# Memory attention of a two-layer hybrid model: products of rounded operands in place of fp32 ones, values of a head for 512 queries at once

## The reference, cut to what matters

```python
MEM_HEADS = 4; MEM_HEAD_DIM = 256

def memory_attention(h, m, w_q, w_k, w_v, w_o):
    b, s, _ = h.shape
    ml = m.shape[1]
    q = (h @ w_q).reshape(b, s, MEM_HEADS, MEM_HEAD_DIM)
    k = (m @ w_k).reshape(b, ml, MEM_HEADS, MEM_HEAD_DIM)
    v = (m @ w_v).reshape(b, ml, MEM_HEADS, MEM_HEAD_DIM)
    sc = jnp.einsum('bqhd,bkhd->bhqk', q, k).astype(jnp.float32) * (MEM_HEAD_DIM ** -0.5)
    pr = jax.nn.softmax(sc, axis=-1).astype(v.dtype)
    o = jnp.einsum('bhqk,bkhd->bqhd', pr, v).reshape(b, s, D_MODEL)
    return o @ w_o

x = x + memory_attention(rmsnorm(x, norm_mem_q[i]), rmsnorm(mem, norm_mem_kv[i]), w_mq[i], w_mk[i], w_mv[i], w_mo[i])
```

## Time and profile before

| | before |
|---|---|
| median of 3 runs | 3662.88 us (3661.35 to 3664.59) |
| the profiled execution, its time | 3663.21 us |
| its span, first to last instruction | 3661.4 us |
| TensorE busy (matmul) | 3595.0 us, 98% |
| VectorE busy | 2130.7 us, 58% |
| ScalarE busy | 1832.3 us, 50% |
| GpSimd busy | 1836.9 us, 50% |
| mean granted clock of TensorE | 0.996 |

### The profile page before, as it was taken

One profiled execution on the slowest core, in us unless ns is written; L12 is line 12 of the kernel. 1 busy time (PEld: TensorE's weight loads), 2 busy tenths in 40 slices (PEclk: granted clock), 3 DMA queues, 4 the chain that ended last, 5 costly groups with the idle time before them and its releaser, 6 DMA issues.

```text
span 3661.4 us, 58169 instructions
## 1 busy us (share of the span) xinstructions
PE 3595.0 (98%) x19482; PEld 2943.8 (80%) x19482; DVE 2130.7 (58%) x3276; ACT 1832.3 (50%) x3521; POOL 1836.9 (50%) x1579
## 2 busy tenths in 40 slices
PE   9999999999999989999999999999999999999999
PEld 7877788888887767888888887788888997678887
DVE  6576642788635766427886664742236977743234
ACT  5656444444445664444434645844445753754443
POOL 3424573556544245735555763265564235245563
PEclk9999999999999999999999999999999999999999
DMA  4211241465322112414653422132223552012222
GB/s 150 91 64 41 81 144 58 161 192 188 104 91 86 65 41 82 145 62 160 191 191 113 139 92 93 59 104 95 94 97 112 176 173 81 2 58 90 95 97 87
DMA packets 106912, 388.58 MB, mean 106 GB/s; under 512 B 11856, under 2 KB 11984, under 8 KB 106320
## 3 DMA queue, kind: packets, MB, share of 16 engines
q1 hardware_dynamic: 87840, 318.81, 26.2%
q10 hardware_dynamic: 16416, 57.62, 4.7%
...
...
## 4 chain that ended last, share of the span: by engine, by line
PE 74%; issue 13%; POOL 7%; DVE 3%; ACT 1%; DMA 0%; POOLq 0%; DVEq 0%; ACTq 0%
PE ps L713 18%; PE ps L715 18%; PE ps L714 18%; POOL arena_parts L656 4%; PE ps L1215 2%; PE ps L2522 2%; PE ps L2545 2%; POOL arena_parts L666 2%; PE ps L2510 1%; PE ps L1234 1%; PE ps L1223 1%; POOL lines L440 1%; PE ps L1193 1%; PE ps L978 1%; PE ps L956 1%
## 5 line engine op out<-in xcount | busy, mean ns | idle before, releaser
L714 PE MATMUL ps<-arena_parts 128*128 128x512 f32 (+1 forms) x3148 | 1171.3, 372 | 0.0
L656 POOL TENSOR_TENSOR arena_parts<-ring,arena_parts 128x512 fp32r<-128x512 f32 x506 | 671.1, 1326 | 805.0 <-ACT arena_parts L633 798.6
L666 POOL TENSOR_TENSOR arena_parts<-ring,arena_parts 128x512 fp32r<-128x512 f32 x506 | 684.5, 1353 | 294.1 <-ACT arena_parts L642 293.3
L713 PE MATMUL ps<-h_parts,arena_parts 128*128 128x512 f32 x2080 | 814.6, 392 | 1.4 <-DVE arena_parts L563 1.2
L715 PE MATMUL ps<-h_parts,arena_parts 128*128 128x512 f32 x2080 | 809.4, 389 | 0.0
L1872 DVE SCALAR_TENSOR_TENSOR conv<-ps,cols,conv 128x511 f32<-128x511 f32 (+3 forms) x536 | 377.5, 705 | 535.2 <-ACT conv L1887 387.3
L714 PEld LDWEIGHTS ps<-arena_parts 128*128 128x128 f32 x3148 | 594.4, 189 | 104.1 <-issue 2.4
L633 ACT ACTIVATE arena_parts<-ring 128x512 fp32r<-128x512 f32 x574 | 360.2, 628 | 605.2 <-PE ps L715 572.8
L642 ACT ACTIVATE arena_parts<-ring 128x512 fp32r<-128x512 f32 x574 | 359.9, 627 | 590.2 <-PE ps L715 549.2
L713 PEld LDWEIGHTS ps<-h_parts,arena_parts 128*128 128x128 f32 x2080 | 390.5, 188 | 86.1 <-issue 3.3
L715 PEld LDWEIGHTS ps<-h_parts,arena_parts 128*128 128x128 f32 x2080 | 390.5, 188 | 81.7
...
## 6 DMA issues: line engine op xcount, KB each, us to landing
...
```

What stands on the lines that cost most here:

```text
L656: eng.tensor_tensor(side_of(lin, i, c, 0, to), side_of(lin, i, c, 0, raw), side_of(lin, i, c, 0, top), ALU.subtract)\
L666: eng.tensor_tensor(side_of(lin, i, c, 1, to), side_of(lin, i, c, 1, raw), side_of(lin, i, c, 1, top), ALU.subtract)\
L713: pe.matmul(out, w_h, x_h, start=start, stop=False)
L714: pe.matmul(out, w_h, x_r, start=False, stop=False)
```

## The change

1. Keys, values, queries and turned probabilities are held as high part (fp32r) and rest. ScalarE's copies write the high part and count `m_high`; VectorE then makes the rest from PSUM and counts `lin_free` (`memory_rest_dve`). The rests lie in space that is free at the time (`hc`, `sq`, `arena`, `conv`).
2. Scores of a unit are 2 x `three` products of 256 columns. A unit's turned probabilities are copied by ScalarE as high part, and VectorE makes the rest (`rest_of_prob`, new semaphore `pt_rest`).
3. The values of a head are made once for its 512 queries: 4 x `three` products of 512 columns, when its last block is turned and split, in TensorE's step n = 5, 9, 13 (heads 0, 1, 2). Before, they were made for each unit.
4. The scores of units 0 and 1, their softmax and the first normalisation run ahead of the last query chunk (`mem_first_*`). Unit 2's scores wait until all eight query chunks have their rest.
5. The values of head 3 stand in `mo`'s first chunk, ahead of k = 6.

```diff
-        m_q = cut(4096, KD, SEQ)
-        m_k = cut(8192, KD, MEM)
-        m_v = cut(10240, 2, DM)
+        m_q, mq_rest = cut_parts(4096, KD, SEQ), cut_parts(12288, KD, SEQ)
+        m_k, mk_rest = cut_parts(8192, KD, MEM), hc_parts
+        m_v, mv_rest = cut_parts(10240, 2, DM), sq_parts[:, :, :].rearrange("p a b -> p (a b)").rearrange("p (t n) -> p t n", t=2)
+        m_probT = [(cut_parts(16384, 2, SEQ), cut_parts(17408, 2, SEQ)), (conv_parts[:, 0:2, :], conv_parts[:, 2:4, :])]
...
+        def mem_scores(pe, l, un):
+
+            wait(pe, "p_done", un.at - 1)
+            pe.wait_ge(S["lin_free"], L["mq", l].chunk0 + 2 if un.nth % MEM_UNITS < 2 else L["mq", l].freed)
+            for c in range(2):
+                k = 2 * un.hd + c
+                mm = three(pe, un.scores, m_q[:, k, un.qs], mq_rest[:, k, un.qs], m_k[:, k, :], mk_rest[:, k, :], c == 0, c == 1)
+            mm.then_inc(S["sc_done"], 1)
+
+        def mem_values(pe, l, hd):
+
+            pe.wait_ge(S["pt_ready"], U_MEM[l] + (hd + 1) * QB)
+            pe.wait_ge(S["pt_rest"], l * MEM_UNITS + (hd + 1) * QB)
+            if hd >= 2:
+                pe.wait_ge(S["mo_evac"], l * MEM_HEADS + hd - 1)
+            p_high, p_rest = m_probT[hd % 2]
+            for c in range(2):
+                cs = slice(hd * 256 + c * P, hd * 256 + (c + 1) * P)
+                for kb in range(2):
+                    mm = three(pe, ps[:, 2 * (hd % 2) + c, :], m_v[:, kb, cs], mv_rest[:, kb, cs], p_high[:, kb, :], p_rest[:, kb, :], kb == 0, kb == 1)
+            mm.then_inc(S["pv_done"], QB)
...
+            for n, un in enumerate(units):
+                if n > QB and n % QB == 1:
+                    mem_values(pe, l, n // QB - 1)
+                if n + 2 < MEM_UNITS:
+                    mem_scores(pe, l, units[n + 2])
+                turn(un)
...
+            def rest_of_prob(un):
+                dve.wait_ge(S["pt_ready"], un.at + 1)
+                dve.tensor_tensor(un.rest, un.turned, un.high.bitcast(F32), ALU.subtract).then_inc(S["pt_rest"], 1)
...
+            for n in range(1, MEM_UNITS + 2):
+                if 2 <= n < MEM_UNITS:
+                    mem_top_dve(dve, units[n])
+                if 2 <= n <= MEM_UNITS:
+                    mem_inverse_dve(dve, units[n - 1])
+                if n >= 2:
+                    rest_of_prob(units[n - 2])
+                if n >= 2 * QB and n % QB == 0:
+                    out(n // QB - 2)
             out(MEM_HEADS - 1)
...
+            for n in range(1, MEM_UNITS + 1):
+                if 2 <= n < MEM_UNITS:
+                    mem_exps_act(act, units[n])
+                copy(units[n - 1])
+                if n >= 7 and n % QB == 3:
+                    out(n // QB - 1)
             out(MEM_HEADS - 1)
...
-                linear_pe(pe, L["mq", l], pair_of(HP, rest_of(rest_mq)), SEQ, n["mq"].split, after=banks_of(L["mv", l], MEM // P))
-                att_pe(pe, mem_pass(l), 0, 0, 0, True, True)
-                linear_pe(pe, L["mo", l], pair_of(of(o_high), HP), SEQ, lambda k: [("mo_evac", l * MEM_HEADS + max(k // 2, MEM_HEADS - 2) + 1)])
+                linear_pe(pe, L["mq", l], pair_of(HP, rest_of(rest_mq)), SEQ, n["mq"].split, after=banks_of(L["mv", l], MEM // P),
+                          hook=hooks(c5=lambda: mem_first_pe(pe, l)))
+                mem_pe(pe, l)
+                linear_pe(pe, L["mo", l], pair_of(of(o_high), HP), SEQ, lambda k: [("mo_evac", l * MEM_HEADS + max(k // 2, MEM_HEADS - 2) + 1)],
+                          midway=(KD - 2, lambda: mem_values(pe, l, MEM_HEADS - 1)))
...
-                split_dve(dve, n["mq"], X, lambda k: col(("mq_norm", l), k), HP, rest_of(rest_mq))
+                memory_keys_dve(dve, l, 0, 1)
+                inverse_dve(dve, n["mq"])
+                memory_keys_dve(dve, l, 2, 3, 4)
+
+                def between(k):
+                    if 1 <= k <= 3:
+                        memory_keys_dve(dve, l, k + 4)
+                    elif k == KD - 1:
+                        memory_values_dve(dve, l, 0)
+                split_dve(dve, n["mq"], X, lambda k: col(("mq_norm", l), k), HP, rest_of(rest_mq), before=between, inverse=False)
+                memory_values_dve(dve, l, 1)
+                memory_queries_dve(dve, l, *range(KD - 1))
+                mem_first_dve(dve, l)
+                memory_queries_dve(dve, l, KD - 1)
                 mem_dve(dve, l)
```

223 lines of the change are left out of this document (76 added, 147 removed).

## The result

The changed kernel takes **3681.8 us** at the median of 5 runs (3680.6 to 3685.0), against 3662.9 before: a ratio of 1.0047 (estimated over all runs of both), 95% interval 1.0036 to 1.0058. By the medians it is slower by 18.9 us. The forecast was 3674.9, its range 3667 to 3685; so the sign and the range hold, and the forecast is 6.9 us too low. The profiled execution has a span of 3680.2 us where the one before had 3661.4.

A forecast was written before the change was run, and what follows sets the result against it. TensorE, busy 98%, was taken to bound the kernel; a longer chain through the other engines adds 11.4 us over both layers, plus 0.6 leak, 12.0 on about 3663: 3674.9 us, range 3667 to 3685.

The forecast's parts named there:

- wait for the query rest: Before unit 2's scores, TensorE waits 2.26 us until VectorE has made the rest of all query chunks.
- first values: The first head's values may start 7.99 us after the last query product's slot ends, after four VectorE rounds.
- head period: From one head's values to the next: a chain through three engines takes 8.93 us, against 7.92 before.
- first output product: The output linear mo starts at 33.61 us, after waiting for the output rest of head 2.
- seventh block, at full clock: mo's k = 6 starts at 43.02 us, after waiting 2.51 us for head 3's output.
- longer in a layer: The attention stage up to mo's k = 6 takes 44.46 us instead of 38.76, 5.7 us longer.
- the exponential and the multiply: TensorE idle about 1 us before scores 10 and 14 (exponential), 0.9 us before transposes 8 and 12.
- work decides: Rival: VectorE and ScalarE keep ahead, a head takes TensorE's 6.49 us, kernel faster at 3650 us; chance 0.06.
- the products are as cheap as the rows of before said: Rounded-operand products take 0.12 us at 256 columns, 0.227 at 512; rival that they cost more, chance 0.02.
- the leak of 0.3 us a layer in the key and value rests: VectorE's key and value rests delay ScalarE's weight halves: 0.3 us a layer, bounds 0 and 1.7.
- the clock, given 0.14 as a rival: Rival: TensorE's idle waits make the clock fall once in each layer, adding 6.8 us, 3681.7 in all; chance 0.14.
- half clock in the stage: Sign of being wrong: the granted clock shows 0.5 in the attention stage.

The follow-up runs named there:

- e1_busy: Changed kernel plus products that compute nothing used, filling TensorE's waits ahead of the output product and behind the last head's values; 3677.2 us, 1.0034 of the kernel before.
- e3_late: Changed kernel with each head's output copy and rest one or two units later in ScalarE's and VectorE's queues; 3674.1 us, 1.0032 of the kernel before.
- e2_tail: Changed kernel with the last head's values ahead of the output product and head 2's output behind the last probability copies and rests; 3668.4 us.
- e7_first: Changed kernel with the first two scores, exponentials and sums behind the last query block on all three engines; 3680.9 us, 1.0043 of the kernel before.
- e9_later: Changed kernel with e2_tail's and e3_late's moves, scores awaiting own head's queries, two waits filled, values and output copies later, values behind scores; 3655.9 us.
- e10_half: Changed kernel with a head's values in two blocks of 256 queries, two units apart, instead of one of 512; 3669.1 us, 1.0016 of the kernel before.

## Why the prediction was right or wrong

**Right: TensorE bounded the stage before, and the change put a chain in its place.** The terms of the sum against the trace, first layer, from the slot's end at 569.56:

| step of the prediction | predicted | measured |
|---|---|---|
| two score groups in the queries | 1.44 | 1.43 (562.66 to 564.09) |
| rest of probabilities, 128x256 | 0.42 | 0.42 |
| wait for the query rest | 2.26 | 2.24 |
| first values | 7.99 | 7.96 |
| head period | 8.93 | 8.99, 8.95 |
| first output product | 33.61 | 33.71 |
| seventh block, at full clock | 43.02 | 43.13 (e1_busy, 615.75 less 572.62) |
| longer in a layer | 5.7 | 5.8 |

Every wait it named is in the trace. Those for the exponential and the multiply are shorter than it said (0.72 and 0.62, not about 1 and 0.9), and the one of 1.90 ahead of the output product has no releaser in the trace; VectorE's output rest of head 2 ends 0.1 us before it does (601.94 and 1.23 long, against 603.27), which fits the cause it gave. e3_late, e2_tail and e7_first each took away or put back one of them and moved the seventh block by 3.3, 3.6 and 1.1 us, within 0.2 us of what the same durations give.

**Right: the rival "work decides" falls.** e3_late moves no work and gains 3.3 us a layer. But what that rival hoped for can be had: e9_later reaches a period of 7.05 with the same instructions in another order, and fillers beside them. That the products are as cheap as the rows of before said is right too.

**Not seen: the leak of 0.3 us a layer in the key and value rests.** From the norm's inverse to the first query product it is 42.19 us before and 42.22 after, so the term was nothing. Span times clock still differs by 12 us where the stage explains 11.6; the remaining half microsecond is below what these figures can tell.

**Wrong: the clock, given 0.14 as a rival and left out of the sum.** This is the step that failed. The sum without it, 12.0 us, is what the runs show at full clock (3657 less 3645); the measured 18.9 has some 7 us more. The rival's price (6.8 us, 3681.7 in all) is what came, but that it fits so closely is luck. It had one fall of 3.4 us in each layer, and the trace has two in each, one around the output product's start and one right behind the wait of 2.37 inside it, the wait nearest to the case that the prediction knew. The prediction's own sign of being wrong, half clock in the stage, came true.

The reasoning took each wait alone, set 2.5, 2.3 and 2.0 us between or beside a wait of 2.11 that kept its clock and one of 2.70 that did not the earlier trace rows, and called a fall unlikely. Neither of the two is a bound. That wait of 2.11 stands in the profile of every kernel here; in four (before, after, e2_tail, e10_half) the clock stayed at 1.00 behind it, in the other nine it fell. The stretch of the earlier trace rows, in e3_late:

```profile
344.00:350.00 6.00, 3.89 (x33) 3.15 (x32) 2.46 (x9) 1.20 (x3) 2.66 (x4) 0.75 0.21 77
```

TensorE is busy for the same 3.89 us and waits the same 2.11, at a clock of 0.75 and not 1.00. One trace showed one of two outcomes, and the forecast read it as a bound. The trace of before also had a shorter wait with a fall behind it, which the forecast did not look at: this one of 1.59 us, with 0.83 in 400 to 420 (the row shown above).

```profile
402.21 1.40 PE L460 MATMUL ps<-const,lines 128*128 128x1 f32 x8 [1.59 <-DVE lines L440]
```

At the place of the wait of 2.70 (about 1405 us) the wait is 1.6 us in six of the thirteen profiles and 2.7 in the others, and the clock falls in it or within 2.1 us behind it in all. So the length of a wait, by these traces, does not say whether the clock stays.

The Trainium skill (TensorE: Matmul & The Clock Gate, Why this matters for your kernels) was cited for idle gaps in mid-kernel. Here the trace agrees that idle time costs the clock, but the waits are shorter than the gap of over about 3 us that it names: 1.59 and 2.70 in the kernel before, and in e2_tail the clock fell in the second layer (0.91 in 1600 to 1620) with no wait over 1 us behind the one at the start of the attention. Another section of that page, A second HAM failure mode: psum-queue depth-cycling, tells of frequent short idling between groups of matmuls under which the clock goes up and down, and that is nearer to this case; no run here separates the two.

**What stays open** is where exactly a fall comes. The two layers of e2_tail and of e3_late have equal waits and unequal clocks (1.00 and 0.91; 1.00 and 0.83), and the first layers of the changed kernel and of e7_first have equal waits and equal busy time ahead of the output product and unequal clocks (0.94 and 1.00 in the 8 us shown there). The runs don't tell what else decides it.
